# Layer 1 opens with the input's rotary queries instead of the memory's keys

## What is computed

```python
for l in range(DEPTH):
    y = hybrid_mixer(rms_norm(h, mix_norm_pre[l]), positions, w_in[l], ...)
    h = h + rms_norm(y, mix_norm_post[l])
    y = memory_cross_attention(rms_norm(h, x_norm_pre[l]), rms_norm(mem, mem_norm[l]), x_wq[l], x_wk[l], ...)
    h = h + rms_norm(y, x_norm_post[l])
    y = conv_ffn(rms_norm(h, ffn_norm_pre[l]), w_up[l], ...)
    h = h + rms_norm(y, ffn_norm_post[l])
```

## Time and profile before

| what | us |
|---|---|
| median of 3 runs | 843.61 (842.57 to 843.74) |
| the profiled execution, its own time | 842.91 |
| its span, first to last instruction | 840.9 |
| TensorE busy | 819.4 |
| DVE busy | 616.2 |
| ACT busy | 498.6 |

### The profile page before, as it was taken

One profiled execution on the slowest core, in us unless ns is written; L12 is line 12 of the kernel. 1 busy time (PEld: TensorE's weight loads), 2 busy tenths in 40 slices (PEclk: granted clock), 3 DMA queues, 4 the chain that ended last, 5 costly groups with the idle time before them and its releaser, 6 DMA issues.

```text
span 840.9 us, 12988 instructions
## 1 busy us (share of the span) xinstructions
PE 819.4 (97%) x5152; PEld 731.8 (87%) x5152; DVE 616.2 (73%) x1080; ACT 498.6 (59%) x765; POOL 28.4 (3%) x53
## 2 busy tenths in 40 slices
PE   2999999999999999999999999999999999999997
PEld 2898898889889999998899889888988899999885
DVE  5679996574685987886577899848467488878653
ACT  4564877565556666564454578656565566665441
POOL 2000000010010000000020000001000000000000
PEclk9999999999999999999999999999999999999999
DMA  9655443564374565556647543456635636655661
GB/s 342 224 176 173 127 140 115 168 228 153 125 231 146 154 199 186 169 195 225 191 145 253 182 151 104 148 170 177 229 102 173 203 101 201 201 179 170 207 195 50
DMA packets 40651, 147.31 MB, mean 175 GB/s; under 512 B 4560, under 2 KB 4688, under 8 KB 40592
## 3 DMA queue, kind: packets, MB, share of 16 engines
q1 hardware_dynamic: 38432, 138.90, 51.8%
q0 software_dynamic: 2160, 7.59, 2.8%
HBM read 145.43 MB, written 1.05 MB: 174 GB/s over the span
## 4 chain that ended last, share of the span: by engine, by line
PE 87%; DVE 7%; ACT 2%; DMA 2%; issue 2%; POOL 0%; SPq 0%; DVEq 0%; POOLq 0%; ACTq 0%
PE acc L1385 7%; PE acc L1387 7%; PE acc L1386 7%; PE acc L1425 4%; PE acc L1427 3%; PE acc L1370 3%; PE acc L1426 3%; PE acc L1368 3%; PE acc L1369 3%; PE psAB L1370 3%; PE psAB L1369 3%; PE psAB L1368 3%; PE psCD L1385 3%; PE psCD L1387 3%; PE psCD L1386 3%; DVE arena L1107 3%
## 5 line engine op out<-in xcount | busy, mean ns | idle before, releaser
L834 DVE TENSOR_TENSOR wlo<-raw,whi 128x1024 fp32r<-128x1024 f32 x240 | 289.6, 1222 | 90.3 <-ACT whi L481 88.2
L481 ACT ACTIVATE whi<-raw 128x1024 fp32r<-128x1024 f32 x240 | 249.9, 1056 | 115.9 <-PE acc L1370 45.3
L1385 PE MATMUL acc<-xT_hi,whi 128*128 128x256 f32 x432 | 123.2, 285 | 0.0
L1386 PE MATMUL acc<-xT_lo,whi 128*128 128x256 f32 x432 | 122.2, 283 | 0.0
L1387 PE MATMUL acc<-xT_hi,wlo 128*128 128x256 f32 x432 | 122.2, 283 | 0.0
L1385 PEld LDWEIGHTS acc<-xT_hi,whi 128*128 128x128 f32 x432 | 82.8, 192 | 2.8 <-issue 2.7
L1386 PEld LDWEIGHTS acc<-xT_lo,whi 128*128 128x128 f32 x432 | 82.8, 192 | 0.2
L1387 PEld LDWEIGHTS acc<-xT_hi,wlo 128*128 128x128 f32 x432 | 82.8, 192 | 0.0
L1385 PE MATMUL psCD<-xT_hi,whi 128*128 128x256 f32 x192 | 54.6, 285 | 0.0
L1387 PE MATMUL psCD<-xT_hi,wlo 128*128 128x256 f32 x192 | 54.3, 283 | 0.0
L1386 PE MATMUL psCD<-xT_lo,whi 128*128 128x256 f32 x192 | 54.3, 283 | 0.0
(11 more groups left out here) (275 smaller groups left out, 2015.3 us busy)
## 6 DMA issues: line engine op xcount, KB each, us to landing
raw<-stream_dram SPq DMA_DIRECT2D x256, 512.0 KB, 4.2
gpre<-gain_dram POOLq DMA_DIRECT2D x7, 512.0 KB, 5.8
gpost<-gain_dram POOLq DMA_DIRECT2D x6, 512.0 KB, 5.4
memn<-mem_dram SPq DMA_DIRECT2D x2, 512.0 KB, 6.0
h<-x_dram SPq DMA_DIRECT2D x1, 1024.0 KB, 12.2
out_dram<-h SPq DMA_DIRECT2D x4, 256.0 KB, 2.1
cst<-const_dram SPq DMA_DIRECT2D x1, 896.0 KB, 16.6
gpre<-gain_dram SPq DMA_DIRECT2D x1, 512.0 KB, 5.2
```

The costliest lines, as they stand in the source:

```text
L481: act.activation(home(g)[0], raw[:, s * GW:(s + 1) * GW], ACT.Copy).then_inc(w_hi.sem, 1)
L834: dve.tensor_tensor(lo, raw[:, cols], hi.bitcast(F32), ALU.subtract).then_inc(w_lo.sem, 1)
L1385: pe.matmul(dst, whi[:, cols], hi[:, toks], start=k == 0 and c % 2 == 0, stop=False)
L1386: pe.matmul(dst, whi[:, cols], lo[:, toks], start=False, stop=False)
```

## The change

In layer 1 alone, the order of the first products becomes queries, convolution, memory's keys, then the transposes of the rotated queries; layer 2 keeps its order. `load_order` permutes the first twelve groups to match, and `first_groups` gives the positions. The queries' product is taken apart into passes (a pass is one of the three matmul kinds over one group and one row tile) in a written order. x and positions are loaded first, in two tiles; memory is normed during layer 1's first products; its gain, `par`, `pww`, the post gain and most of the constants are loaded later. A new tile `idle` is set to zero by DVE, and TensorE multiplies it with itself 24 times, and 5 times more behind the first transposes; the results aren't used. ACT runs one sine on a single column at its start. The scaling of memory for layer 2 moves to the output projection. The rotation of the queries moves behind the convolution's gate, the first eight taps are cut in other pieces.

```diff
@@ -71,8 +71,15 @@
 
 def load_order(g):
 
+    if g < G_DLK:
+        return (g + PER_TILE) % G_DLK
     u = g % GROUPS - G_UP
     return g if not 0 <= u < 2 * HELD else g + (HELD if u < HELD else -HELD)
+
+
+def first_groups(layer):
+
+    return (G_WK0, G_DLQ, G_CV) if layer else (2 * PER_TILE, 0, PER_TILE)
 
...
         @block.sync
         def _(sp_):
-            tiles = lambda a: a.rearrange("(t p) n -> p t n", p=P)
+            def group(g):
+                slot = g % RING
+                sp_.dma_start(raw[:, slot * GW:(slot + 1) * GW], stream[load_order(g)]).then_inc(raw_in[slot].sem, 16)
+
+            def x_rows(t):
+                sp_.dma_start(h[:, t * D:(t + 1) * D], x[t * P:(t + 1) * P, :]).then_inc(x_in[t].sem, 16)
+
+            sp_.dma_start(posi[:, :], pos).then_inc(pos_in.sem, 16)
             sp_.dma_start(cst[:, 0:CC_TRI], consts[:, 0:CC_TRI]).then_inc(head_in.sem, 16)
+            x_rows(0)
+            group(0)
+            sp_.dma_start(gpre[:, :], gains[0, MIX_PRE, :].partition_broadcast(P)).then_inc(gain0_in.sem, 16)
+            group(1)
+            x_rows(1)
+            group(2)
+            group(3)
             sp_.dma_start(memn[:, 0:D], mem[0:P, :]).then_inc(mem0_in.sem, 16)
-            sp_.dma_start(gpre[:, :], gains[0, MEM_G, :].partition_broadcast(P)).then_inc(mgain_in.sem, 16)
             sp_.dma_start(memn[:, D:2 * D], mem[P:2 * P, :]).then_inc(mem1_in.sem, 16)
-            for s in range(2):
-                sp_.dma_start(raw[:, s * GW:(s + 1) * GW], stream[s]).then_inc(raw_in[s].sem, 16)
-            sp_.dma_start(h[:, :].rearrange("p (t n) -> p t n", t=TOK), tiles(x)).then_inc(x_in.sem, 16)
-            for s in range(2, RING):
-                sp_.dma_start(raw[:, s * GW:(s + 1) * GW], stream[s]).then_inc(raw_in[s].sem, 16)
-            sp_.dma_start(cst[:, CC_TRI:CC], consts[:, CC_TRI:CC]).then_inc(cst_in.sem, 16)
             for g in range(RING, DEPTH * GROUPS):
-                s = g % RING
                 sp_.wait_ge(w_lo.sem, g + 1 - RING)
-                sp_.dma_start(raw[:, s * GW:(s + 1) * GW], stream[load_order(g)]).then_inc(raw_in[s].sem, 16)
+                group(g)
+                if g == 2 * RING:
+                    sp_.dma_start(cst[:, CC_TRI:CC], consts[:, CC_TRI:CC]).then_inc(cst_in.sem, 16)
...
-                pool.wait_ge(mem_ms.sem, mem_ms.at(0, t - TOK + 1))
-                rsqrt(S_HRS + t, S_HMS + t).then_inc(mem_rs.sem, 1)
-
-            pool.wait_ge(mg_done.sem, mg_done.at(0, 0))
-            gain(gpre, gpre_in, 0, MIX_PRE)
 
             def before_sub_layer(l, i, t):
                 pool.wait_ge(h_ms.sem, h_ms.at(l, TOK * i + t + 1))
@@ -430,6 +439,14 @@
 
             for t in range(TOK):
                 before_sub_layer(0, 0, t)
+            pool.wait_ge(xn_ready.sem, xn_ready.at(0, 2 * TOK))
+            gain(gpre, gpre_in, 0, MEM_G)
+            for t in range(TOK):
+                pool.wait_ge(mem_ms.sem, mem_ms.at(0, t - TOK + 1))
+                rsqrt(S_MRS + t, S_MMS + t).then_inc(mem_rs.sem, 1)
+            load_params(0)
+            gain(gpost, gpost_in, 0, MIX_POST)
+            pool.wait_ge(mg_done.sem, mg_done.at(0, 0))
 
...
+            def squares_x(t):
+                act.wait_ge(x_in[t].sem, 16)
+                for n in range(2):
+                    cols = slice(t * D + n * NT, t * D + (n + 1) * NT)
+                    act.activation(junk[:, cols], h[:, cols], ACT.Square, accum_out=st(S_HSQ + 2 * t + n)).then_inc(h_sq.sem, 1)
+
...
+
+            act.wait_ge(half_set.sem, 1)
+            own.link(act.activation(junk[:, 0:1], st(S_POW), ACT.Sin))
+            squares_x(0)
+            split_group(0, 0)
             act.wait_ge(trig_arg.sem, 1)
             act.activation(trig[:, :], trig[:, :], ACT.Sin).then_inc(trig_ready.sem, 1)
-            split_group(0, 0)
-            for t in range(TOK):
-                memory_hi(0, t, -2 * TOK)
+            first_input_hi(0, 0)
             split_group(0, 1)
-            act.wait_ge(x_in.sem, 16)
-            for t in range(TOK):
-                squares_h(0, 0, t)
-            for g in range(2, RING):
-                split_group(0, g)
+            squares_x(1)
+            first_input_hi(0, 1)
+            split_group(0, 2)
+            split_group(0, 3)
+            for b in range(2):
...
+                g_wk0, g_dlq, g_cv = first_groups(l)
+                if l:
+                    input_hi(0, 0)
+                    split(6)
+                    transposed_in(KT[:, 0:4 * SEQ], psAB, g_wk0 + PER_TILE, KT_in)
+                    split(g_dlq + PER_TILE - 1)
+                    input_hi(0, 1)
+                else:
+                    for t, landed in enumerate((mem0_in, mem1_in)):
+                        squares_memory(t, landed)
+                    split(g_cv + PER_TILE)
+                    memory_hi(0, 0, -2 * TOK)
+                    split(g_cv + PER_TILE + 1)
+                    memory_hi(0, 1, -2 * TOK)
+                split(g_cv + PER_TILE - 1 + AHEAD)
+                act.wait_ge(w_used.sem, w_used.at(l, g_cv + PER_TILE))
...
                 act.activation(sig, accs[1][1][:, :], ACT.Sigmoid).then_inc(cv_sig.sem, 1)
-                columns(dqT, q_tr, dqT_in)
+                if l:
+                    columns(dqT, q_tr, dqT_in)
+                else:
+                    split(g_cv + PER_TILE + AHEAD)
...
+                if not l:
+                    split(g_wk0 + PER_TILE - 1 + AHEAD)
+                    transposed_in(KT[:, 0:4 * SEQ], psAB, g_wk0 + PER_TILE, KT_in)
+                    columns(dqT, q_tr, dqT_in)
...
-            dve.wait_ge(mem_sq.sem, mem_sq.at(0, 1 - TOK))
-            mean_square(S_HMS, S_HSQ).then_inc(mem_ms.sem, 1)
             for c in (part1, part2, part3):
...
+            def first_scale(t, n):
+                cols = slice(t * D + n * NT, t * D + (n + 1) * NT)
+                dve.wait_ge(gain0_in.sem, 16)
+                dve.wait_ge(h_rs.sem, t + 1)
+                dve.scalar_tensor_tensor(xn[:, cols], h[:, cols], st(S_HRS + t),
+                                         gpre[:, n * NT:(n + 1) * NT], ALU.mult, ALU.mult).then_inc(xn_ready.sem, 1)
+
+            def first_input_lo(t, b):
+                dve.wait_ge(xt_hi.sem, 2 * t + b + 1)
+                dve.tensor_tensor(chunks(xT_lo, b, t), blocks(psCD[b]), chunks(xT_hi, b, t).bitcast(F32),
+                                  ALU.subtract).then_inc(xt_lo.sem, 1)
+
+            norm_input(0, 0, 0)
+            first_scale(0, 0)
+            split_group(0, 0)
+            first_input_lo(0, 0)
+            first_scale(0, 1)
+            split_group(0, 1)
+            norm_input(0, 0, 1)
+            first_input_lo(0, 1)
+            split_group(0, 2)
+            for n in range(2):
+                first_scale(1, n)
+            split_group(0, 3)
+            for b in range(2):
+                first_input_lo(1, b)
...
+                else:
+                    dve.memset(gpad[:, :, 0:CV_K - 1], 0.0).then_inc(gpad_zero.sem, 1)
+                    split(4)
+                    for t in range(TOK):
+                        dve.wait_ge(mem_sq.sem, mem_sq.at(0, t + 1 - TOK))
+                        mean_square(S_MMS + t, S_YSQ + t).then_inc(mem_ms.sem, 1)
+                    split(5)
+                    memory_scale(0)
+                    split(6)
+                    memory_scale(1)
+                    split(g_cv + PER_TILE)
+                    memory_lo(0, 0, -2 * TOK)
+                    split(g_cv + PER_TILE + 1)
+                    memory_lo(0, 1, -2 * TOK)
+                    dve.wait_ge(par_in.sem, par_in.at(l, 0))
+                split(g_cv + PER_TILE - 1 + AHEAD)
...
                                   sig.rearrange("p (c n) -> p c n", c=2), ALU.mult).then_inc(gpad_in.sem, 1)
-                conv_taps(1, 4)
-                split(G_DLK + AHEAD)
-                conv_taps(4, 6)
-                split(G_DLK + 1 + AHEAD)
-                conv_taps(6, 8)
-                split(G_DLK + 2 + AHEAD)
-                conv_taps(8, 9)
-                split(G_DLK + 3 + AHEAD)
+                if l:
+                    conv_taps(1, 4)
+                    split(G_DLK + AHEAD)
+                    conv_taps(4, 6)
+                    split(G_DLK + 1 + AHEAD)
+                    conv_taps(6, 8)
+                    split(G_DLK + 2 + AHEAD)
+                    conv_taps(8, 9)
+                    split(G_DLK + 3 + AHEAD)
+                else:
+                    split(g_wk0 + AHEAD)
+                    rope(0, qr, g_dlq + PER_TILE, q_roped)
+                    split(g_wk0 + 1 + AHEAD)
+                    conv_taps(1, 3)
+                    split(g_wk0 + 2 + AHEAD)
+                    conv_taps(3, 5)
+                    split(g_wk0 + 3 + AHEAD)
+                    conv_taps(5, 7)
+                    split(G_DLK + 1 + AHEAD)
+                    conv_taps(7, 9)
+                    split(G_DLK + 3 + AHEAD)
```

(94 more changed lines are left out.)

60 lines of the change are left out of this document (25 added, 35 removed).

## The result

The changed kernel takes 834.81 us (834.56 to 834.92), the kernel before 843.66 beside it: the ratio is 0.9902, interval 0.989 to 0.9914, 8.85 us less. The profiled execution took 834.92 with a span of 832.5, 8.4 us shorter than the span of before. The prediction said 835.8, in 834.0 to 840.0.

What follows compares the result with a forecast made beforehand. TensorE bounds the kernel behind its opening; an earlier, full-pace start moves the first rotary-key matmul from 57.98 to 49.7, 8.3 less 0.5 gives 7.8 us gain: 835.1 profiled, plus 0.7 for the median, 835.8 us; range 834.0 to 840.0.

Steps and rivals of the forecast that it cites:

- the mark: First matmul of the rotary keys (DLK): from 57.98 to 49.7 us by the sum, gain cut by 0.5 to 7.8.
- Behind the mark: TensorE's program after the first rotary-key matmul: the same as before, every stage as long as before.
- Loads: Opening loads on SP's queue: x tile 0 lands at 5.2 us, group 0 at 6.4, mixer gain at 7.9.
- The lower bound: Positions' load on SP taken as 2.0 us, so DVE's sine arguments end at 6.4, hidden behind ACT's squares.
- the upper one: Positions' load taking 4.0 us: sine arguments end at 7.9, first operand 0.9 us later, gain 6.9 instead of 7.8.
- The rule of small transfers: Transfers below 512 B are read, modified and written; positions, 8 bytes a partition, go first; cost on SP unknown.
- The zeros: 24 products on zeros before the first turn: 4.5 us at half pace (10.7 products), end 8.85, turn at 8.9.
- The queries: TensorE's passes and turns from 10.5 us, with waits of 1.1, end the queries' product at 23.85.
- Behind the queries: Nothing on the path: group 4 has 0.45 us of slack, the memory gain 3 us.
- A: Products on zeros don't lift the clock in time: 4.0 us lost, 839.8 us; chance 12%.
- B: Memory gain lands late, at 34, turn at 35.4 instead of 29.6: 6 us lost, 841.8 us; chance 4%.
- C: Memory gain lands beyond 35.8, each us further a net loss; 845.6 us at 21 us after issue; chance 4%.

Runs made afterwards that it cites:

- POOL's load: The changed kernel with positions loaded by POOL as before, not first on SP: 835.80 us.
- the late taps: The changed kernel with layer 1's first eight taps put behind the split of group 15, in the pieces of before, instead of under memory's keys: 836.89 us.
- the plain passes: The changed kernel with the queries' product done group by group, all three passes of a group together, as before: 836.37 us.

## Why the prediction was right

- **The bound.** Right: TensorE's time from the mark on is the same work, and each experiment that moved the mark moved the end of its span by as much, to 0.2 us. The same work didn't take the same time everywhere, though (see "Behind the mark").
- **Loads.** Right in order, each 0.4 to 0.6 us too early: x tile 0 landed 3.9 us after its issue at 1.65, so at 5.55 (5.2), group 0 at 6.9 (6.4), the mixer gain at 8.5 (7.9). I had taken x tile 0's landing as that of the first memory tile, but it is issued 0.47 later; the time from issue to landing was the same 3.9.
- **Positions.** The lower bound was the right choice, and the upper one was priced rightly: 0.9 forecast, 1.1 at the mark with POOL's load. The rule of small transfers named there changed nothing that can be seen: DVE waited for the constants behind them.
- **The zeros.** Half pace lasted from 1.46 to 7.16 us, 13 products, where I had allowed 4.5 us and 10.7. They ended at 9.7 and not at 8.85 (the whole row of 24 took 8.42 us, the sum has 7.5). The page prints a granted clock of 1.00 for this stretch; the pace of 0.43 us for 512 columns is the 1.2 GHz level. The turn came 0.8 later than forecast (9.71, 8.9). But no one number would have been right: from one execution to the next the rise came after 9 to 14 products (see the last section), and 10.7 lies inside. It also cost less than it looks, since the late gain alone would have put the turn at 9.3 to 9.7: the scaled half was there at 9.24 in this trace, and with twenty products, and again with the late taps, the zeros ended early and the turn waited for the scaling until 9.62 and 9.72.
- **The queries.** 25.13 for 23.85: 0.8 from the turn, the rest the joints between passes, transposes and waits. The waits were where I had put them: for ACT's split of group 2, DVE's of the same group, and the copy of tile 1.
- **Behind the queries.** Right: no wait on group 4, whose low half was ready at 24.99 for a use at 25.13. That is 0.14 us of slack where I had 0.45. The first query group was given back later than forecast, and ACT, done with memory's squares at 21.6, waited 1.08 us for it. The memory gain landed at 24.6 and had about the 3 us that I counted: a delay of 2.5 cost nothing.
- **The mark.** 49.7 by the ledger, 50.2 with the half microsecond taken off; measured 50.70. Gain to the mark 7.3 for 7.8.
- **Behind the mark.** Wrong: I said that every stage would be as long as before, and one was shorter by 1.1 us. I had listed the taps' new place, and asked only whether DVE would be late by it; the wait list's small entries had told me that nothing was lost there before. That list can't show it, nor can a busy share: matmuls that run one after another count as busy just as those side by side. So 835.8 is 1.0 from the measured 834.8 partly by luck, through two errors of opposite sign: 0.5 us of gain too much at the mark and 1.1 too little behind it. The 0.4 us that are left are how the profiled executions lie to their medians.
- **Rivals.** A did not come about: the clock rose 2.5 us before the first turn. Taking the zeros out altogether costs 1.9. That the rise shifts from run to run is so: the row of 24 zeros took 7.66 to 8.64 us. B and C were not met, but their mechanism holds, and C was under-priced by the 1.9 us that the lower clock costs. Whether B's shorter wait would lower the clock too was not tried. The landing from which C said that nothing is won, 35.8, came out all the same (35.9 gave 843.05 against 842.89), because the turn that it counts from was forecast at 29.6 and came at 30.9: again two errors that cancel.

Where the 8.85 us come from: about 1.1 behind the mark (DVE in time for both heads), 0.9 to 1.9 the clock, 1.6 the order of passes, some 1.0 positions ahead on SP. These overlap. The rest, 3 to 4 us, is put down to the order itself, x and its queries ahead of memory. That part is what is left over and not measured: it wasn't tried apart from the order of the loads, since the one needs the other.

## What to carry to other kernels

When one engine is full from its first product to its last, count what its first instruction needs, and let it start on a quarter of its input; then the passes should follow the order in which the operands are made. Products on zeros are worth as much as the real work they keep at full pace: about 1 us here with a late start and 2 us with an early one. A list of waits and a busy share both miss products that run one after another where they could run side by side: lay the two traces side by side, matmul by matmul, and the same loss may be found in a later layer, where it can be won again.

## What was not expected of the hardware

A gain load that held TensorE for 6.05 us, and put its turn 6.4 us late, cost 8.2 us: the granted clock stood at 0.50 for the next 4.3 us of work, over which eight transposes took 1.97 us and matmuls of 256 columns 0.21 us each. Waits of 0.78 us (in the trace without the five products) and of 1.14 us left the pace as it was.

The moment of the rise is not the kernel's alone. In twelve traces TensorE starts on the same zeros at 1.46 us, and half pace ends between 5.6 us (after 9 products) and 7.6 us (after 14). TensorE's first row of 24 zeros with the late taps, in the changed kernel, and with the plain passes:

```profile
1.46 7.66 PE L1448 MATMUL acc<-idle 128*128 128x512 f32 x24 [1.46 <-DVE idle L874]
```

```profile
1.46 8.42 PE L1449 MATMUL acc<-idle 128*128 128x512 f32 x24 [1.46 <-DVE idle L874]
```

```profile
1.46 8.64 PE L1449 MATMUL acc<-idle 128*128 128x512 f32 x24 [1.46 <-DVE idle L874]
```

Up to there TensorE's program is the same in all three. In the kernel without zeros half pace lasted 4.9 us from its first transpose (9.55 to 14.5). In the kernel before it lasted from the first transpose at 9.92 to 21.9, with waits of 3.52 and 1.41 us in between. A count of products taken from one execution can't be relied on in another.
